# Mixture of experts: the first block for counts over 64 is computed third instead of second

## The chip, the cores and the metric

The kernel runs on one core of a Trainium2 chip. The metric is the device time of one execution in microseconds (us), the median of several runs. One execution more was recorded by the hardware profiler; the rows below come from it. The engines are TensorE (PE: matmuls and transposes), VectorE (DVE), ScalarE (ACT), GpSimd (POOL) and SyncE (SP); SP and POOL each issue transfers into a queue of their own, and 16 DMA engines serve both.

## The reference, cut to what matters

Two blocks of a language model run one after the other on 512 tokens of 1024 features. The change touches one part of the second, the mixture of experts. Each token goes to the 2 best of 8 experts of its best group, of 32 experts in all; an expert is a small gated network with 256 hidden features.

```python
def hierarchical_moe(h, w_rg, b_rg, w_re, b_re, w_gate, w_up, w_down):
    hf = h.reshape(-1, d)
    ...
    expert_id = g_sel[:, None] * EXPERTS_PER_GROUP + top_i
    combine = jnp.sum(jax.nn.one_hot(expert_id, N_EXPERTS, dtype=jnp.float32)
                      * (g_w * top_p)[..., None], axis=1)
    y = jnp.zeros_like(hf)
    for grp in range(N_GROUPS):
        sl = slice(grp * EXPERTS_PER_GROUP, (grp + 1) * EXPERTS_PER_GROUP)
        hid = jax.nn.silu(jnp.einsum('td,edf->tef', hf, w_gate[sl])) * jnp.einsum('td,edf->tef', hf, w_up[sl])
        y = y + jnp.einsum('tef,efd->td', hid * combine[:, sl, None].astype(hid.dtype), w_down[sl])
    return y.reshape(b, s, d)
```

## The kernel before

512 tokens with 2 experts each are 1024 pairs. The kernel sorts them by expert and gathers all their rows into `xs` before the first expert (four times two gathers `rows_a`, `rows_b`). The expert stage then works on windows of 64 pairs (`SLOTS`). Two windows are computed together as one step, one in each half of TensorE's output: a *main* step n computes the first 64 pairs of expert n and of expert n + 16. If an expert has more than 64 pairs, the rest goes into a block of an *over* step; over step o holds blocks o and o + 8 of a list that is filled from the front. For the inputs here two experts have more than 64 pairs (17 with 65, 19 with 67), so block 0 (in over step 0) and block 1 (in over step 1) are real, both in the first half of their step, and the other 14 are empty. All 24 steps are always run: 16 main ones (`M0` to `M15` below) and 8 over ones (`O0` to `O7`). `STEPS` is their order: M0 O0 M1 M2 O1 M3 M4 O2 M5 and so on.

A step s has these parts. `up(s)` multiplies the window with gate and up weights, in two halves c = 0 and c = 1 that have a weight panel each per window; ACT and DVE make the hidden rows from it (`xsg`, `xhid`), `turn_hid(s)` turns them with two transposes, ACT copies them (`xturn`), and `down_moe(s)` multiplies with the down weights (c = 2). ACT copies the result into `y_out`, which has two buffers, and POOL's `store_y(s)` scatters it to DRAM. TensorE's order is up(s), down(s - 1), turn(s); only at the start it is up(0), up(1), turn(0), down(0), turn(1).

The weights come as panels of 1 MB (128 x 2048 floats). Main panels, six per main step, come through SP's queue into a ring of nine buffers, in the order `PANEL_ORDER` that `_panel_order` builds from `STEPS`: the four up panels of step s, then the two down panels of step s - 1. The first nine are loaded before the stage begins; after that SP waits before panel n until `main_used` counts n - 8 panels used, so panel n takes the place of panel n - 9. Panel numbers start from 0.

Over panels come through POOL's queue, as indirect loads, one per half: `load_over(q)` with q = 3 * o + c loads part c of over step o for both halves into the buffer pair q % 2. For q of 2 and more it first waits for `over_used` to reach 2 * q - 2, that is until part q - 2 has been used. For an empty block only one row is in bounds, and the other rows are skipped. POOL executes its waits, loads and stores strictly in their written order. Before the stage it issues loads 0 and 1; then, after the table `y_row` is ready, the order that the change rewrites. ACT waits before it writes `y_out` of step s until the store of step s - 2 has landed.

After the last step POOL gathers the results (`back`), and the last part of the block follows.

Of the kernel before, what the change touches and what calls it, by code (L numbers as in the profile page):

```python
# [42 lines left out]
XOVER = 16  # L43
# [5 lines left out]
NO_WEIGHT = 16384  # L49


STEPS = [(kind, n) for o in range(XOVER // 2) for kind, n in (("main", 2 * o), ("over", o), ("main", 2 * o + 1))]
NSTEP = len(STEPS)
PANELS = 9


def _panel_order():

    up_at, down_at, order = {}, {}, []
    for s in range(NSTEP + 1):  # L60
        if s < NSTEP and STEPS[s][0] == "main":
            up_at[s] = len(order)
            order += [(STEPS[s][1] + XHALF * half, c) for c in range(2) for half in range(2)]
        if s and STEPS[s - 1][0] == "main":
            down_at[s - 1] = len(order)
            order += [(STEPS[s - 1][1] + XHALF * half, 2) for half in range(2)]
    return up_at, down_at, order
# [9 lines left out]
def column(s):  # L77

    kind, n = STEPS[s]
    return n if kind == "main" else XHALF + n  # L80
# [118 lines left out]
def build(nc, x_t, p_t, w_p, w_a, w_b, w_m, small, const, rope, decay, distance, out_t):  # L199
    ctx = ExitStack()  # L200
    with ctx:
# [2940 lines left out]
        def _(pool):  # L3142
# [80 lines left out]
            def load_over(q):  # L3223

                o, c = q // 3, q % 3
                if q >= 2:
                    pool.wait_ge(over_used, 2 * q - 2)
                for half in range(2):
                    j = half * (XOVER // 2) + o
                    pool.indirect_dma_start(  # L3230
                        over_panel[half][q % 2][:, :], None, w_m.rearrange("a p n -> (a p) n"),
                        bass.IndirectOffsetOnAxis(ap=over_row[:, c, j:j + 1], axis=0),
                        bounds_check=3 * EXPERTS * P - 1, oob_is_err=False).then_inc(over_loaded[half][q % 2], 16)

            def store_y(s):
                c = column(s)
                pool.wait_ge(y_copied, s + (2 if s == NSTEP - 1 else 1))
                pool.indirect_dma_start(
                    y_dram[:, :], bass.IndirectOffsetOnAxis(ap=y_row[:, c:c + 1], axis=0), y_out[:, s % 2, :], None,
                    bounds_check=PAIRS + XBLOCKS - 1, oob_is_err=False).then_inc(y_stored[s % 2], 16)  # L3240
# [16 lines left out]
            load_over(0)  # L3257
            load_over(1)
            pool.wait_ge(tables_ready, 5)
            for s in range(NSTEP):  # L3260
                kind, o = STEPS[s]
                if kind == "over":
                    load_over(3 * o + 2)
                    if o + 1 < XOVER // 2:
                        load_over(3 * o + 3)
                    store_y(s - 1)
                    if o + 1 < XOVER // 2:
                        load_over(3 * o + 4)
                    store_y(s)
                    store_y(s + 1)  # L3270
            pool.wait_ge(xwa_ready, NSTEP)
            pool.wait_ge(xwb_ready, NSTEP)
            for v in range(2):
# [208 lines left out]
```

## Time and profile before

| | |
|---|---|
| median of 3 runs | 2145.59 us (2143.97 to 2146.25) |
| profiled execution: time | 2143.46 us |
| profiled execution: span, first to last instruction | 2141.6 us |
| mean granted TensorE clock | 0.998 of full speed |
| busy: PE, PE weight load, DVE, ACT, POOL | 98%, 74%, 59%, 39%, 13% |
| expert stage, first up to last down | 1791.9 to 2062.9 us |

The time of the profiled execution is to be compared with its span: 1.9 us lie outside the recorded instructions. All times in rows are us from the start of the span. Matmuls are pipelined, so the end of one can lie behind the start of the next, and a few records of matmuls are missing (an up of 16 matmuls shows as 32 records of passes). In the expert stage L1413 is the matmul of `up`, L1424 that of `turn_hid`, L1437 that of `down_moe`, L3230 the load of an over panel and L3238 the store of a result.

### The profile page before, as it was taken

Reading aid. Unit: us, or ns where it says so; the run is one execution under the profiler, and the core shown is the slowest. Engines: PE = TensorE matmul, PEld = TensorE weight load, DVE = VectorE, ACT = ScalarE, POOL = GpSimd, SP = SyncE. Lnnn points to the kernel's source line nnn. Section 1 sums busy time; section 2 is a strip of 40 time slices with the busy share of each in tenths; the row PEclk is TensorE's granted clock in tenths of the full one; section 3 lists DMA queues with packets and bytes.
Section 4 is the critical chain, followed back from the end, with each engine's and each line's share of the span. In section 5 each row is a group of like instructions: output and inputs, shape, how many; then the busy total and the mean of one; then the engine's idle time right before and its main releaser. Section 6 shows DMA issues by size and latency. Waiting matters only on the chain.

```text
span 2141.6 us, 27223 instructions
## 1 busy us (share of the span) xinstructions
PE 2095.6 (98%) x10474; PEld 1578.0 (74%) x10474; DVE 1267.6 (59%) x1704; ACT 836.0 (39%) x1258; POOL 271.3 (13%) x234
## 2 busy tenths in 40 slices
PE   8999999999999999999999999999999998999998
PEld 6787788888878877888888888877778884333346
DVE  7887855555587678875655555588775454000038
ACT  6556522222253445774422222264552232122143
POOL 1334200000010064000100000020000023222220
PEclk9999999999999999999999999999999999999999
DMA  5322322223214352112322222221122158999961
GB/s 204 123 95 73 118 97 100 88 88 118 78 64 155 124 170 79 36 40 89 131 99 104 91 88 93 93 71 62 65 99 90 68 232 323 418 414 398 395 235 60
DMA packets 62622, 298.13 MB, mean 139 GB/s; under 512 B 14080, under 2 KB 14464, under 8 KB 34582
## 3 DMA queue, kind: packets, MB, share of 16 engines
q1 hardware_dynamic: 42560, 261.60, 31.9%
q0 software_dynamic: 19552, 34.55, 5.2%
q8 instruction: 63, 1.03, 0.2%
q10 hardware_dynamic: 416, 0.70, 0.1%
q14 instruction: 31, 0.25, 0.0%
HBM read 326.37 MB, written 22.48 MB: 163 GB/s over the span
## 4 chain that ended last, share of the span: by engine, by line
PE 79%; DVE 9%; DMA 6%; ACT 3%; issue 2%; POOL 1%; POOLq 0%; ACTq 0%; DVEq 0%
PE psum L652 21%; PE psum L654 21%; PE psum L653 21%; PE psum L1413 5%; DMA panel<-w_m 4%; PE psum L1437 3%; PE psum L1102 2%; PE psum L1077 1%; DVE a_lo L2137 1%; ACT a_hi L1520 1%; DMA over_panel<-w_m,over_row 1%; DVE xc L2294 1%; DVE hs L2248 1%; ACT hn_hi L1547 0%; PE psum L1235 0%
## 5 line engine op out<-in xcount | busy, mean ns | idle before, releaser
L652 PE MATMUL psum<-hn_hi,a_hi 128*128 128x512 f32 (+1 forms) x1592 | 628.4, 395 | 1.9 <-DVE a_lo L2126 0.9
L654 PE MATMUL psum<-hn_hi,a_lo 128*128 128x512 f32 (+1 forms) x1592 | 618.7, 389 | 0.0
L653 PE MATMUL psum<-hn_lo,a_hi 128*128 128x512 f32 (+1 forms) x1592 | 618.4, 388 | 0.0
L652 PEld LDWEIGHTS psum<-hn_hi,a_hi 128*128 128x128 f32 (+1 forms) x1592 | 297.2, 187 | 74.0 <-issue 8.2
L653 PEld LDWEIGHTS psum<-hn_lo,a_hi 128*128 128x128 f32 (+1 forms) x1592 | 297.4, 187 | 64.8 <-issue 2.4
L654 PEld LDWEIGHTS psum<-hn_hi,a_lo 128*128 128x128 f32 (+1 forms) x1592 | 297.0, 187 | 64.3
L2137 DVE TENSOR_TENSOR a_lo<-a_raw,a_hi 128x2048 fp32r<-128x2048 f32 (+2 forms) x108 | 247.3, 2290 | 69.4 <-ACT a_hi L1520 68.9
L1520 ACT ACTIVATE a_hi<-a_raw 128x2048 fp32r<-128x2048 f32 (+2 forms) x108 | 201.4, 1866 | 71.0 <-PE psum L654 61.8
L2236 DVE TENSOR_TENSOR h<-h,psum 128x512 f32<-128x512 f32 x176 | 119.4, 687 | 78.4 <-PE psum L654 78.4
L3150 POOL TENSOR_TENSOR sq<-sq 128x512 f32<-128x512 f32 x5 | 7.8, 1555 | 1121.6 <-ACT sq L1533 1121.6
L3072 DVE TENSOR_TENSOR xhid<-xsg,psum 128x256 f32<-128x256 f32 x24 | 10.1, 422 | 231.3 <-ACT xsg L2081 231.3
L1701 ACT ACTIVATE sg<-sg 128x512 f32<-128x512 f32 x44 | 27.8, 633 | 286.3 <-DVE sg L2407 286.3
L652 PE MATMUL psum<-hid_hi,b_hi 128*128 128x512 f32 x352 | 137.3, 390 | 2.2 <-DVE h L2236 2.1
L654 PE MATMUL psum<-hid_hi,b_lo 128*128 128x512 f32 x352 | 137.0, 389 | 0.0
L653 PE MATMUL psum<-hid_lo,b_hi 128*128 128x512 f32 x352 | 137.0, 389 | 0.0
L1413 PE MATMUL psum<-panel,xw 128*64 128x512 f32 x512 | 113.4, 595 | 0.0
L2412 DVE TENSOR_TENSOR hid<-sg,psum 128x512 f32<-128x512 f32 x44 | 30.3, 688 | 113.8 <-PE psum L654 113.6
L1703 ACT ACTIVATE hid_hi<-hid 128x512 fp32r<-128x512 f32 x44 | 27.8, 632 | 177.5 <-DVE hid L2412 177.5
L1527 ACT ACTIVATE b_hi<-b_raw 128x1024 fp32r<-128x1024 f32 x64 | 67.0, 1051 | 65.4 <-PE psum L654 63.2
L1413 PEld LDWEIGHTS psum<-panel,xw 128*64 128x64 f32 x512 | 35.3, 137 | 66.9 <-issue 66.5
L2143 DVE TENSOR_TENSOR b_lo<-b_raw,b_hi 128x1024 fp32r<-128x1024 f32 x64 | 79.8, 1254 | 1.0 <-ACT b_hi L1527 1.0
L652 PEld LDWEIGHTS psum<-hid_hi,b_hi 128*128 128x128 f32 x352 | 66.1, 188 | 17.5 <-issue 2.6
(533 smaller groups left out, 3257.2 us busy)
## 6 DMA issues: line engine op xcount, KB each, us to landing
a_raw<-w_a SPq DMA_DIRECT2D x115, 1024.0 KB, 5.1
panel<-w_m SPq DMA_DIRECT2D x96, 1024.0 KB
b_raw<-w_b SPq DMA_DIRECT2D x64, 512.0 KB, 3.4
q_scratch<-q_hi POOLq DMA_DIRECT2D x7, 384.0 KB
q_scratch<-qb_lo POOLq DMA_DIRECT2D x7, 384.0 KB
q_hi<-q_scratch POOLq DMA_DIRECT2D x7, 384.0 KB
q_lo<-q_scratch POOLq DMA_DIRECT2D x7, 384.0 KB
token_rows<-nat POOLq DMA_DIRECT2D x4, 512.0 KB, 5.4
```

The costliest lines, as they stand in the source:

```text
L652: pe.matmul(out, w_hi, x_hi, start=first, stop=False)
L653: pe.matmul(out, w_hi, x_lo, start=False, stop=False)
L654: return pe.matmul(out, w_lo, x_hi, start=False, stop=last)
L1102: mm = pe.matmul(bank[6 + at % 2][side * DV:(side + 1) * DV, t * P:(t + 1) * P], w, x, start=i == 0, stop=i == len(steps) - 1)
L1413: mm = pe.matmul(bank[v][rows, :], xw[:, v, k, rows], w[half][:, k % 4 * 2 * EFF:(k % 4 + 1) * 2 * EFF], start=k == 0, stop=k == KT - 1)
L1437: mm = pe.matmul(bank[4 + 2 * v + hb][rows, :], xturn[:, v, f * P + half * SLOTS:f * P + (half + 1) * SLOTS], w[half][:, f * D + hb * 512: ...
L1520: act.activation(a_hi[s % 2][:, 0:w], a_raw[s % 2][:, 0:w], ACT.Copy).then_inc(a_rounded, 1)
L1527: act.activation(b_hi[s % 2][:, :], b_raw[s % 2][:, :], ACT.Copy).then_inc(b_rounded, 1)
L2137: V.tensor_tensor(a_lo[s % 2][:, 0:w], a_raw[s % 2][:, 0:w], a_hi[s % 2][:, 0:w], ALU.subtract) \
L2143: V.tensor_tensor(b_lo[s % 2][:, :], b_raw[s % 2][:, :], b_hi[s % 2][:, :], ALU.subtract) \
L2236: V.tensor_tensor(h[:, m, :], h[:, m, :], bank[4 + m % 4][:, :], ALU.add).then_inc(y_free, 1)
L2412: V.tensor_tensor(hid[:, f, :], sg[:, f, :], ps[1][:, :], ALU.mult).then_inc(tile_free, 2)
```

## The change

The first over step comes as the third step of the stage, after M0 and M1, and no longer between them. The order becomes M0 M1 O0 M2 O1 M3 M4 O2 and so on: all other steps keep their places. The order of the main panels follows from `STEPS`. POOL's order is written anew, since the stores no longer come in threes: every load keeps its place relative to its over step (loads 3o + 2 and 3o + 3 before the store of the step ahead of it, load 3o + 4 behind that store), and the stores are counted up in between. All rows are still gathered before the first step.

```diff
-STEPS = [(kind, n) for o in range(XOVER // 2) for kind, n in (("main", 2 * o), ("over", o), ("main", 2 * o + 1))]
+STEPS = [("main", 0), ("main", 1), ("over", 0)] + [
+    (kind, n) for o in range(1, XOVER // 2) for kind, n in (("main", 2 * o), ("over", o), ("main", 2 * o + 1))]
 NSTEP = len(STEPS)
 PANELS = 9
@@
             load_over(0)
             load_over(1)
             pool.wait_ge(tables_ready, 5)
-            for s in range(NSTEP):
-                kind, o = STEPS[s]
-                if kind == "over":
-                    load_over(3 * o + 2)
-                    if o + 1 < XOVER // 2:
-                        load_over(3 * o + 3)
-                    store_y(s - 1)
-                    if o + 1 < XOVER // 2:
-                        load_over(3 * o + 4)
-                    store_y(s)
-                    store_y(s + 1)
+            over_at_step = [s for s in range(NSTEP) if STEPS[s][0] == "over"] + [NSTEP + 1]
+            at = 0
+            for o in range(XOVER // 2):
+                s, following = over_at_step[o:o + 2]
+                while at < s - 1:
+                    store_y(at)
+                    at += 1
+                load_over(3 * o + 2)
+                if o + 1 < XOVER // 2:
+                    load_over(3 * o + 3)
+                store_y(at)
+                at += 1
+                if o + 1 < XOVER // 2:
+                    load_over(3 * o + 4)
+                while at < following - 1:
+                    store_y(at)
+                    at += 1
```

POOL's order at the start was, after loads 0 and 1: load 2, load 3, store M0, load 4, store O0, store M1, load 5, load 6, store M2, load 7, store O1, store M3. It becomes: store M0, load 2, load 3, store M1, load 4, store O0, load 5, load 6, store M2, load 7, store O1, store M3.

## Rows read from the trace of the kernel before

**Rows 1.** The page: span, chain that ended last by line, issues of main panels.
```profile
span 2141.6 us, 27223 instructions
...
PE psum L652 21%; PE psum L654 21%; PE psum L653 21%; PE psum L1413 5%; DMA panel<-w_m 4%; PE psum L1437 3%; PE psum L1102 2%; PE psum L1077 1%; DVE a_lo L2137 1%; ACT a_hi L1520 1%; DMA over_panel<-w_m,over_row 1%; DVE xc L2294 1%; DVE hs L2248 1%; ACT hn_hi L1547 0%; PE psum L1235 0%
...
panel<-w_m SPq DMA_DIRECT2D x96, 1024.0 KB
```

**Rows 2.** Expert stage by windows: stretch, PE busy (records), PE clock, DMA share, GB/s.
```profile
1791.90:2062.90 271.00, 261.64 (x1202) 1.00 0.96 389
```

**Rows 3.** Timeline of PE, expert stage: start, length, line, what, [idle before <-releaser].
```profile
1791.88 7.09 PE L1413 MATMUL psum<-panel,xw 128*64 128x512 f32 x32
1798.80 3.60 PE L1413 MATMUL psum<-over_panel,xw 128*64 128x512 f32 x16
1802.94 3.65 PE L1413 MATMUL psum<-over_panel,xw 128*64 128x512 f32 x16 [0.54 <-DMA over_panel<-w_m,over_row]
1806.53 0.44 PE L1424 MATMUL psum<-cn,xhid 128*128 128x128 f32 x2
1807.44 3.65 PE L1437 MATMUL psum<-panel,xturn 128*64 128x512 f32 x16 [0.47 <-ACT xturn L2052]
...
1818.31 3.60 PE L1437 MATMUL psum<-over_panel,xturn 128*64 128x512 f32 x16
...
1833.03 7.09 PE L1413 MATMUL psum<-over_panel,xw 128*64 128x512 f32 x32
...
1843.85 7.09 PE L1413 MATMUL psum<-panel,xw 128*64 128x512 f32 x32
...
1856.01 7.09 PE L1413 MATMUL psum<-panel,xw 128*64 128x512 f32 x32
...
1897.46 3.65 PE L1437 MATMUL psum<-panel,xturn 128*64 128x512 f32 x16 [1.91 <-DMA panel<-w_m]
...
2032.45 3.65 PE L1437 MATMUL psum<-panel,xturn 128*64 128x512 f32 x16 [1.42 <-DMA panel<-w_m]
```

**Rows 4.** Waits of PE in the expert stage: us in total, times, longest.
```profile
PE psum L1437 <- DMA panel<-w_m: 6.2, 5, 1.9
```

**Rows 5.** DMA queues from 1791.9 to 1897.4: packets, MB, share of 16 engines.
```profile
q1 hardware_dynamic: 4756, 34.71, 79.3%
```

**Rows 6.** DMA queues from 1791.9 to 2032.4 (q1 is SP's queue, q0 POOL's).
```profile
q1 hardware_dynamic: 11895, 86.69, 87.2%
```

**Rows 7.** DMA queues from 1842 to 1847.
```profile
q1 hardware_dynamic: 148, 1.08, 51.6%
q0 software_dynamic: 148, 1.04, 49.8%
```

**Rows 8.** DMA queues from 1847 to 1850.
```profile
q0 software_dynamic: 165, 0.04, 6.5%
```

**Rows 9.** Chain that ended last, at M3: start, us, what.
```profile
1838.89 13.03 DMA over_panel<-w_m,over_row
```

**Rows 10.** DMA queues from 1838 to 1842.
```profile
q0 software_dynamic: 131, 0.38, 23.9%
```

**Rows 11.** Timeline of POOL: issues of loads (L3230) and stores (L3238), with idle before.
```profile
1793.64 0.99 POOL L3230 DMA_INDIRECT over_panel<-w_m,over_row  x1 [0.30 <-issue]
...
1813.01 1.02 POOL L3238 DMA_INDIRECT expert_out<-y_out,y_row  x1 [2.75 <-ACT y_out L2062]
...
1822.75 1.01 POOL L3230 DMA_INDIRECT over_panel<-w_m,over_row  x1 [8.71 <-PE psum L1437]
...
1834.63 1.00 POOL L3238 DMA_INDIRECT expert_out<-y_out,y_row  x1 [8.23 <-ACT y_out L2062]
...
1837.55 1.04 POOL L3230 DMA_INDIRECT over_panel<-w_m,over_row  x1 [1.92 <-PE psum L1413]
```

**Rows 12.** Timeline of PE at an idle stretch of another stage.
```profile
1452.48 0.88 PE L1224 MATMUL psum<-wpt,sv 128*64 128x128 f32 x12 [2.33 <-ACT wpt L1934]
```

**Rows 13.** Windows just behind it: PE busy (records), PE clock, DMA share, GB/s.
```profile
1453.50:1456.50 3.00, 3.00 (x11) 0.50 0.01 3
```

## The prediction, made before the change was run

> **What bounds the kernel now.** I read four views in this order: the page, the expert stage's windows and PE timeline, the waits, and the DMA queues by stretch. The page shows a kernel that TensorE fills; panels enter the last chain with 4% and over panels with 1% (span 2141.6 us) [rows 1]. The change touches only the expert stage. It lasts 271.0 us at full clock, with DMA at 0.96 of its time [rows 2]: TensorE and the weight stream are nearly even there. I call the main steps M0 to M15 and the steps for counts over 64 O0 to O7. A step has an up (two halves, c0 and c1), a turn and a down; PE's order is up of a step, down of the one before, turn. An undisturbed step is 10.82 us (O1's up at 1833.03, M3's at 1843.85), of which the up is 6.92 (1791.88 to 1798.80) and the rest 3.90 [rows 3]. 24 such steps are 259.7 us, so the stage loses 11.3 us. 6.2 of them are five waits for main panels, each before the down of an odd main step from M5 to M13 [rows 4].
>
> Which DMA engine is waited for matters. Panel 39 (M5's last; the first nine are loaded beforehand) ends the wait at 1897.46, when the queue has moved 34.71 MB, 33.1 panels of 1024 KB or 1.049 MB, though 39 is only the 31st. At 2032.45 it is the 79th, and 86.69 MB, 82.7 panels, have moved [rows 1, 3, 5, 6]. So a panel counts as landed when the last of the 16 engines is through, two to four panels behind the mean. That last engine needs 135.0 us for 48 panels, 2.81 each or 33.75 per three steps; PE needs 32.46.
>
> **The change, part by part.** *Same work.* No matmul, panel or over block is added; panels 4 to 15 only change places. Panels 4 to 7 become M1's, wanted early and already loaded. The queue goes on with panel 9 at about 1798.5, behind two over loads (2.1 MB, 5 us). At 2.81 us each, panel 9 (M0's down) is there by 1801.5, 11 (M1's down) by 1807, 15 (M2's up, with a store between) by 1820; they are wanted at 1806.6, 1817.5 and 1824.9: no wait. The wait of 0.54 in O0's up goes, since these loads landed at 1802.94 at the latest and O0's up now begins at 1810.6 [rows 3]. I cost it by the starts: M0's down follows its turn by 0.91 as before (1806.53 to 1807.44), and the turn begins at 1798.80 + 6.92 = 1805.72. So M0's down is at 1806.63, O0's up at 1810.58, M1's down at 1817.50, M2's up at 1821.40, O0's down due at 1828.32. With no wait M3's up would stand at 1843.04, 0.8 before its old start.
>
> *The move squeezes the over buffers.* O0 and O1 now have one main step between them, not two. Load q waits until load q-2 has been used. Loads 2, 3 and 4 (O0's c2, O1's c0 and c1) matter. Load 4 takes the buffer of load 2, which is free only after O0's down. That down now stands directly ahead of O1's up, which wants load 4 in its second half, 3.5 us after it begins. Before, M2's up lay between (load 4 was issued at 1822.75, wanted at 1836.5). So a load of 1.05 MB must come inside 4 us, and behind the others on POOL's queue.
>
> What a load costs with main panels queued is shown by load 5. Its full half (O1's first half is a real block, so the block is not empty and the move does what it says) moves 1.04 MB in 5 us while the main queue moves 1.08 [rows 7]; its empty half of small packets takes 3 us more [rows 8]; it lands at 1851.92, 1.9 after that [rows 9]. So 8 us of the queue, 10 to landing. The output store ahead of it, issued at 1834.63, moved 0.38 MB from 1838 to 1842 [rows 10, 11]. The issues follow PE: a store 5.57 us after its down's start (1807.44, 1813.01), a load waiting for a down 4.44 after its start (1818.31, 1822.75), one waiting for c0 4.52 after the up's start (1833.03, 1837.55), one waiting for c1 3.5 later [rows 3, 11]. All of POOL's DMAs up to there:
> - store of M0: issued 1812.2, data to 1820;
> - load 2: issued 1815.1, data 1820 to 1828, landed 1830. O0's down waits 1.7 us;
> - load 3: issued 1818.6, data to 1836, landed 1838. O1's up, due at 1833.9, waits 4 us; c0 ends at 1841.5;
> - store of M1: issued before load 4 now, data to 1840;
> - load 4: issued 1830 + 4.44 = 1834.4, data to 1848, landed 1850. c1 waits 8.5 us.
>
> The other sizing takes issue to landing of load 5 as it stands, 14.4 us [rows 9, 11]: O0's down at 1829.5, load 4 issued at 1833.9 and landed at 1848.3. The lower bound is the load that met no main panels: issued 1793.64, in use at 1802.94, 9.3 us [rows 3, 11]. Above, I allow 3 us more, as a load behind three others is not in the trace.
> The Trainium skill (DMA: Bandwidth & Descriptors, Anatomy of one DMA — SWDGE) puts such a DMA at about 2.0 us plus its bytes over 436e3. That would be an estimated 4.4 us, and load 4 would land at 1838.8; the trace disagrees, with 9.3 and 14.4, and the result by the page is a rival below.
>
> The main queue does stay full: panels 9 to 24 are 16.8 MB, three over loads and two stores 3.9, together 49 us at the 424 GB/s of [rows 7], from about 1798.5 to 1847. Panel 25 must wait for M2's down. Behind PE the ACT and DVE steps of O1, and POOL's store of O0 and load 5, slide along; nothing else waits for them.
>
> *From the landing on:* c1 3.5, M2's down and turn 3.9, so M3's up is at 1857.4 against 1843.85: +13.6. An idle PE also loses its clock: after 2.33 us without work it ran at 0.50 of full, 1.2 instead of 2.4 GHz, for over 3 us, at least 1.5 us of work lost [rows 12, 13]. The cost here is between 0 and 3.5; I take 2: +15.6.
>
> *What is given back.* The waits behind M3's up go while the weights are ahead. Before, M3's up to M4's took 12.16 instead of 10.82 (load 5, 1.34 lost); M4's up to M13's down took 176.44 instead of 15 x 10.82 + 6.92 = 169.22 [rows 3]. That is 8.56 in all. Can the last engine serve it? Panel 25 is issued at about 1859.5, data 2 us later; panel 39 lands at 1861.5 + 15 x 2.81 = 1903.7. PE wants it at 1859.4 + 50.2 = 1909.6. The lead of 6 us shrinks by 1.29 per three steps and at M13 is 0.7: just enough. The end is then that of before.
>
> Sum: 15.6 - 8.6 = +7.0; with the shorter sizing +5.3. I take +6.4, nearer the first, as load 4 has more ahead of it than load 5 had. Against the profiled execution (span 2141.6, time 2143.46, so 1.9 around it) this is 2149.9; its time lies 2.1 below the median of the runs, 2145.59, on which I put the difference: **2152.0 us**.
>
> **Rivals.** By the same sum the result is the landing of load 4 less 1843.0; it decides.
> *The load comes early (not slower).* If the queue serves it as it served the first loads, O0's down is not late, load 4 is issued at 1832.8 and lands at 1842.1. M3's up is at 1849.5, 5.7 us late and 7.7 with the clock, less than the 8.6 that PE gets back. The last DMA engine, which has work until about 1851 (16 panels by 2.81 and three loads by 2.5 from 1798.5) and gets panel 25 before that, is never idle, does the same work as before and sets the end: 2145.6, within 1 us. It holds from a landing before 1847.3 (+4.3). For it: main panels could run low on some engines. Against it: load 5's 14.4 with a shorter queue ahead.
> The page's formula leads here too: load 4 at 1838.8, and no difference.
> *Nothing is given back late.* If the last engine doesn't hold its lead beyond M5, only 1.34 and the 2.07 between M4's up and M5's down (41.45 against 3 x 10.82 + 6.92) return: 15.6 - 3.4 = +12.2, 2157.8 [rows 3]. For it: the lead of 0.7 at M13 is thin. Against: DMA was busy for 0.96 of the stage only [rows 2], so 2.81 per panel may hold idle time.
> *Faster.* The early waits gone (0.8) and the later ones too, would need load 4 within 4.3 us of its issue and a last DMA engine that gains: -4.3 at best, 2141.
>
> **Chances.** Forecast's case (+3.5 to +9) 0.56, early load 0.24, little given back 0.16, faster 0.04. 0.2% is 4.3 us, about what a measurement can tell from no change. Slower by more: most of the forecast's case and all of the third, 0.69; within: 0.27; faster 0.04. The range takes in the early load's edge and the third case: 2146 to 2158.
>
> **What would show it.** Right: PE idle 1 to 3 us before O0's down, then some 3 to 5 us before O1's c0 and 6 to 10 before its c1, both waits ended by an over panel; a stretch at 0.50 clock there; DMA share well below 1 for some 5 us just before panel 25; no wait for a main panel at M5 and M7, or small ones; the stage 277 to 278 us. Wrong: c1 waits less than 4 us; waits of over 1 us for main panels remain at M5 to M13; or new ones appear at M1's or M2's down, which I cost at nothing.

## The result

The changed kernel takes 2150.45 us (median of 6 runs, 2149.93 to 2152.07), the kernel before 2144.39 us in 6 runs on the same chips (2141.10 to 2146.25). The ratio is 1.0034, with a 95% interval of 1.0024 to 1.0043: slower by 6 us by the medians and by 7 us by the ratio. The forecast was 2152.0 us, or +6.4 us, with a range from 2146 to 2158.

The page of the profiled execution (2150.17 us), its span and the chain by line:

```profile
span 2148.4 us, 27223 instructions
...
PE psum L653 21%; PE psum L654 21%; PE psum L655 21%; PE psum L1414 7%; PE psum L1438 4%; PE psum L1103 2%; PE psum L1078 1%; DVE a_lo L2138 1%; DMA over_panel<-w_m,over_row 1%; DMA panel<-w_m 1%; ACT a_hi L1521 1%; DVE xc L2295 1%; PE psum L649 1%; PE psum L1463 1%; DVE hs L2249 1%
```

All lines of the code stand one lower than before (up is L1414, turn L1425, down L1438, over load L3231, store L3239). The chain now hardly goes over main panels (1% after 4%) [rows 1]. The whole difference lies in the expert stage, here as windows:

```profile
1792.20:2069.60 277.40, 264.40 (x1202) 0.98 0.94 380
```

It was 271.0 us at clock 1.00 and DMA share 0.96 [rows 2]. The timeline of PE shows where the time goes:

```profile
1792.18 13.95 PE L1414 MATMUL psum<-panel,xw 128*64 128x512 f32 x64
...
1810.92 7.09 PE L1414 MATMUL psum<-over_panel,xw 128*64 128x512 f32 x32
...
1829.56 3.65 PE L1438 MATMUL psum<-over_panel,xturn 128*64 128x512 f32 x16 [0.73 <-DMA over_panel<-w_m,over_row]
...
1837.06 5.35 PE L1414 MATMUL psum<-over_panel,xw 128*64 128x512 f32 x16 [3.47 <-DMA over_panel<-w_m,over_row]
1848.31 5.42 PE L1414 MATMUL psum<-over_panel,xw 128*64 128x512 f32 x16 [5.90 <-DMA over_panel<-w_m,over_row]
...
1857.47 7.09 PE L1414 MATMUL psum<-panel,xw 128*64 128x512 f32 x32
...
1868.29 7.09 PE L1414 MATMUL psum<-panel,xw 128*64 128x512 f32 x32
...
1907.66 3.60 PE L1438 MATMUL psum<-panel,xturn 128*64 128x512 f32 x16
...
2039.26 3.65 PE L1438 MATMUL psum<-panel,xturn 128*64 128x512 f32 x16 [1.23 <-DMA panel<-w_m]
...
2065.97 3.65 PE L1438 MATMUL psum<-panel,xturn 128*64 128x512 f32 x16 [1.06 <-ACT xturn L2053]
```

The rows are the ups of M0 and M1 together, O0's up, O0's down, the two halves of O1's up, M3's up, M4's up, M5's down, M13's down and M15's down. The stage begins 0.30 us later than before (1792.18 against 1791.88), which is taken off in what follows. M3's up is then 13.3 us late, M4's up 12.0, M5's down 9.9 and M13's down 6.5 [rows 3]; M15's down is 6.5 late too (it was at 2059.17). Three waits and a low clock cost 14.1 us, less the 0.8 us by which an undisturbed M3 would now come earlier, hence 13.3. Half of it is given back: 1.3 us by the wait for load 5 at M3's down, which is gone, and 5.5 us by the waits for main panels, of which one of the five is left [rows 3, 4]. In the waits of PE over the stage:

```profile
PE psum L1414 <- DMA over_panel<-w_m,over_row: 9.4, 2, 5.9
...
PE psum L1438 <- DMA panel<-w_m: 1.2, 1, 1.2
PE psum L1438 <- DMA over_panel<-w_m,over_row: 0.7, 1, 0.7
```

The timeline of POOL, with the store of M0, the first halves of loads 2 and 3, the store of M1 and the first halves of loads 4 and 5:

```profile
1812.61 1.02 POOL L3239 DMA_INDIRECT expert_out<-y_out,y_row  x1 [16.39 <-ACT y_out L2063]
1815.41 1.01 POOL L3231 DMA_INDIRECT over_panel<-w_m,over_row  x1 [1.79 <-PE psum L1414]
...
1818.84 1.00 POOL L3231 DMA_INDIRECT over_panel<-w_m,over_row  x1 [1.11 <-PE psum L1414]
...
1823.36 1.03 POOL L3239 DMA_INDIRECT expert_out<-y_out,y_row  x1 [2.22 <-ACT y_out L2063]
1834.02 1.01 POOL L3231 DMA_INDIRECT over_panel<-w_m,over_row  x1 [9.63 <-PE psum L1438]
...
1843.21 1.01 POOL L3231 DMA_INDIRECT over_panel<-w_m,over_row  x1 [5.54 <-PE psum L1414]
```

Load 4 is held back 9.63 us by O0's down and goes out at 1834.02, beside O1's up that wants it. The windows of PE around the two waits (stretch, PE busy, clock, DMA share, GB/s):

```profile
1838.00:1840.00 2.00, 2.00 (x8) 0.57 1.04 434
...
1846.00:1848.00 2.00, 0.00 (x0) 0.50 1.01 404
...
1850.00:1852.00 2.00, 2.00 (x8) 0.52 0.60 234
1852.00:1854.00 2.00, 2.00 (x12) 1.00 0.08 29
1854.00:1856.00 2.00, 2.00 (x12) 1.00 0.00 0
...
1858.00:1860.00 2.00, 2.00 (x12) 1.00 0.74 258
```

The clock is at 1.2 GHz behind the wait of 3.47 us and again in and behind that of 5.90 us, and each half of O1's up takes 5.3 us where it took 3.5. The Trainium skill (TensorE: Matmul & The Clock Gate, Why this matters for your kernels) warns of such idle gaps between bursts of matmuls; this trace agrees. DMA is nearly idle from 1852 to 1858: the main ring is full up to panel 24, and panel 25 waits for M2's down, as forecast. SP issues panel 25 at 1857.2.

### The profile page after: what moved, and what is told of

Its sections match the earlier page's. It is cut to its first block, busy times and chain, and to the rows that moved or that the text cites. A ratio compares the mean times of both kernels' runs of the same rounds, so it can differ in the third digit from the quotient of the medians.

```text
span 2148.4 us, 27223 instructions
## 1 busy us (share of the span) xinstructions
PE 2099.1 (98%) x10474; PEld 1579.8 (74%) x10474; DVE 1266.9 (59%) x1704; ACT 835.7 (39%) x1258; POOL 270.9 (13%) x234
## 4 chain that ended last, share of the span: by engine, by line
PE 82%; DVE 9%; ACT 3%; DMA 3%; issue 2%; POOL 1%; ACTq 0%; DVEq 0%; POOLq 0%
PE psum L653 21%; PE psum L654 21%; PE psum L655 21%; PE psum L1414 7%; PE psum L1438 4%; PE psum L1103 2%; PE psum L1078 1%; DVE a_lo L2138 1%; DMA over_panel<-w_m,over_row 1%; DMA panel<-w_m 1%; ACT a_hi L1521 1%; DVE xc L2295 1%; PE psum L649 1%; PE psum L1463 1%; DVE hs L2249 1%
## 5 line engine op out<-in xcount | busy, mean ns | idle before, releaser
L1414 PE MATMUL psum<-panel,xw 128*64 128x512 f32 x512 | 113.2, 595 | 0.0
L1414 PEld LDWEIGHTS psum<-panel,xw 128*64 128x64 f32 x512 | 35.4, 137 | 67.2 <-issue 66.9
```

Source lines behind the costliest of these rows:

```text
L1414: mm = pe.matmul(bank[v][rows, :], xw[:, v, k, rows], w[half][:, k % 4 * 2 * EFF:(k % 4 + 1) * 2 * EFF], start=k == 0, stop=k == KT - 1)
```

## Experiments

Every kernel was timed beside the kernel before. "Stage" is the distance from M0's up to M15's down in the profiled execution.

| kernel | median, us | ratio to before (95%) | stage, us |
|---|---|---|---|
| before | 2143.4 to 2144.4 | 1 | 267.3 |
| changed | 2150.45 | 1.0034 (1.0024 to 1.0043) | 273.8 |
| halves_out | 2146.22 | 1.0009 (1.0000 to 1.0018) | 268.9 |
| halves_out_free4 | 2142.26 | 0.9993 (0.9984 to 1.0002) | 267.1 |
| halves_out_free234 | 2140.72 | 0.9986 (0.9977 to 0.9995) | 264.8 |
| before_halves_out | 2141.15 | 0.9989 (0.9980 to 0.9998) | 264.6 |
| warm_wait | 2157.47 | 1.0066 (1.0052 to 1.0079) | 280.4 |
| warm_wait2 | 2148.80 | 1.0023 (1.0014 to 1.0032) | 272.6 |
| hold_main | 2148.75 | 1.0024 (1.0015 to 1.0034) | 272.6 |
| two_between | 2156.29 | 1.0061 (1.0047 to 1.0075) | 279.4 |
| no_empty_before | 2136.05 | 0.9966 (0.9952 to 0.9979) | 259.2 |
| no_empty_after | 2143.41 | 0.9997 (0.9988 to 1.0006) | 267.4 |

The queue theory: the over loads are late, as POOL's queue serves them one after the other, sharing the DMA engines with the main panels. Its rival, the buffer theory: load 4 is late by its buffer alone, with a fixed time from issue to landing. Further rivals: the new order of the main panels costs, or the clock does, or the giving back is a coincidence.

### Queue or buffer: four kernels without the empty second halves

`halves_out` leaves out the second halves of loads 0 to 5 (the blocks are empty, and TensorE computes them with the first half's panel). `over_into` returns None for these halves:

```diff
                 for half in range(2):
+                    b = over_into(q, half)
+                    if b is None:
+                        continue
                     j = half * (XOVER // 2) + o
```

> The changed kernel without the loads of the empty second halves of O0 and O1 (loads 0 to 5; TensorE reads the first half's panel in their place, and rows of empty blocks are not stored). Queue theory (POOL's DMAs to the over buffers are served one after the other at half rate beside main panels, an empty half costing 3 us): load 2 lands before 1828, load 3 before 1833, so the waits of 0.7 and 3.5 us go; load 4, issued at about 1833, lands at about 1843, and its wait is 6 to 7 us from a start 4 us earlier; M3's up at 1850 to 1851.5 instead of 1857.5; time 2144 to 2146.5. Buffer theory (a fixed 14.2 us from issue to landing, and the issue waits for the buffer): load 4 lands at 1847, M3's up at 1854 to 1855, 2147 to 2148.5. If the empty halves cost nothing: as the changed kernel, 2150.5.

Measured: loads 2 and 3 cause no wait any more; the one for load 4 is left:

```profile
1833.18 3.65 PE L1437 MATMUL psum<-over_panel,xw 128*64 128x512 f32 x16
1843.49 6.13 PE L1437 MATMUL psum<-over_panel,xw 128*64 128x512 f32 x16 [6.66 <-DMA over_panel<-w_m,over_row]
```

O1's c0 starts 4.5 us earlier than in the changed kernel and load 4 is used 5.4 us earlier, both from M0's up. It was issued at 1833.71 and used 9.8 us later, not 14.3: the empty halves, its own and those ahead of it in the queue, have a price. The fixed time of the rival is refuted. M3's up is 1 us later than the queue theory had it, since c1 ran at the low clock and took 6.0 us; the time of 2146.22 us lies in that theory's range.

In `halves_out_free4` load 4 goes to the free second-half buffer and waits for nothing:

```diff
+OVER_PLAN = {4: (2, None)}
```

> As halves_out, and load 4 goes to a buffer of its own (that of the left-out second half), so it is issued right behind the store of M1 at about 1824.5 instead of 1833. Buffer theory: the landing moves by the same 8 to 9 us, no wait in O1's second half, M3's up at 1844. Queue theory: its data can only begin when load 3 and the store of M1 are through, about 1834; landed at about 1841, a wait of 3.5 to 5 us, M3's up at 1847 to 1849. Time in both 2143.5 to 2146, as the last DMA engine sets the end; clearly below before (under 2142) would say that it does not.

Measured: POOL issues it 32.5 us after M0's up and no longer 40.9, thus 8.4 us earlier; PE uses it at 47.8 and no longer 50.7, thus 2.9 us earlier.

```profile
1823.12 1.01 POOL L3257 DMA_INDIRECT over_panel<-w_m,over_row  x1 [0.30 <-issue]
```
```profile
1838.40 6.57 PE L1437 MATMUL psum<-over_panel,xw 128*64 128x512 f32 x16 [3.74 <-DMA over_panel<-w_m,over_row]
```

From issue to use it now takes 15.3 us. So the wait for load 4's own buffer is worth 2.9 us here, and a wait of 3.74 us is left that the buffer theory had at nothing: loads 2 and 3, issued as late as in `halves_out`, are still ahead. The time of 2142.26 us is 1 us below what either theory expected. A kernel that has a spare buffer and the second halves as well wasn't tried.

In `halves_out_free234` loads 2 and 3 are issued at 1804, before the store of M0, into buffers of their own, and load 4 behind O0's c0:

```diff
+OVER_PLAN = {2: (2, None), 3: (3, None), 4: (0, 2), 5: (1, 4)}
```

> As halves_out, with buffers for loads 2 and 3 that are free from the start (issued at about 1805, as in the kernel before) and load 4 waiting only for O0's first half (issued at about 1815). Both theories: no wait for an over panel, M3's up at 1843 to 1844, so the whole loss is gone: 2143 to 2145.5. If instead the new order of the main panels cost something of its own, waits for main panels appear at M1's or M2's down and the time stays over 2146.

Measured: no wait for an over panel at all. M3's up is 51.2 us behind M0's, where it is 65.3 in the changed kernel and 52.0 in that before: the 0.8 us that the walk put on the new order are there. The order of the main panels is that of the changed kernel, so it isn't what costs. Nor is the place of O0 by itself: what costs is that loads 2, 3 and 4 are issued too late. Five waits for main panels are back, 5.8 us in all. The time was expected at 2143 to 2145.5 us and is 2140.72. `before_halves_out` is the control, the old order with the same halves left out.

> The kernel before, with the same second halves left out as in halves_out (loads 0 to 5), as the control for the three kernels of that name. Loads 0 and 1 land 1 us earlier and load 5 some 3 us earlier, so the waits of 0.54 and 1.1 go. If the last DMA engine sets the pace, 6 of 44 empty issues less give 1 to 1.5 us: 2142 to 2143.5. Then halves_out_free234 (2140.7) is 1 to 2.5 us faster by the new order alone, in which O0's loads have more time; if the new order were worth nothing, this one comes out at 2140.7 as well.

Measured 2141.15 against 2140.72, stages of 264.6 and 264.8 us. The expectation of 2142 to 2143.5 was too high, and the rival named in it holds: with the loads in time, the place of O0 is worth nothing either way. The 0.8 us early are lost again to main panels. The gain of 2 to 3 us against the kernel before comes from the halves left out, which both kernels share.

### Clock: dummy matmuls in the waits

`warm_wait` puts dummy matmuls ahead of the waits of O1's two halves:

```diff
                     if k % 4 == 0:
+                        if s == 4:
+                            pe.wait_ge(xturn_done, 4)
+                            keep(3, 32 if k else 10)
                         w, used = weights(s, k // 4)
```

> The changed kernel with dummy matmuls (10 and 32 of 128x256) ahead of the two waits of O1's up, so that TensorE is not idle in them. Clock theory: both halves of O1's up take 3.5 us instead of 5.3 and 5.2; the first is hidden by the second's wait, so M3's up comes 1.7 us earlier (1855.8), and so does the request for panel 25; time 2148.5 to 2149.5. If the end hangs on something else, M3's up is earlier but the time stays at 2150.5 and the waits for main panels grow by 1.7. Should the dummy matmuls outlast the wait: up to 1 us later.

Measured: 7 us slower than the changed kernel. A dummy is two records of 0.22 us, and 32 of them last far beyond the landing:

```profile
1841.63 14.08 PE L649 MATMUL psum<-cn 128*128 128x256 f32 x64
1855.64 3.65 PE L1417 MATMUL psum<-over_panel,xw 128*64 128x512 f32 x16
```

The size was wrong, not the idea; both halves of the up take 3.5 us. `warm_wait2` has 5 and 15 in their place.

> As warm_wait, with 5 and 15 dummy matmuls instead of 10 and 32: in warm_wait a dummy took 0.44 us, not 0.22, and 32 of them 14 us, so that TensorE came 8 us too late to load 4. Now 2.2 and 6.6 us, inside the waits. Clock theory: both halves of O1's up at 3.5 us, c0 starting within 0.5 us of the landing of load 3, M3's up 1.5 to 1.8 us earlier than in the changed kernel, time 2148.5 to 2149.5. If the end hangs on something else: 2150.5.

```profile
1840.98 6.74 PE L649 MATMUL psum<-cn 128*128 128x256 f32 x30
1848.83 3.65 PE L1417 MATMUL psum<-over_panel,xw 128*64 128x512 f32 x16 [1.10 <-DMA over_panel<-w_m,over_row]
...
1856.22 7.09 PE L1417 MATMUL psum<-panel,xw 128*64 128x512 f32 x32
```

Load 4 lands at the same time, M3's up comes 1.5 us earlier (63.8 behind M0's) and the stage is 1.2 us shorter. The interval of its ratio overlaps with that of the changed kernel; its middle is 0.0011 lower. The trace shows the low clock as a term of about 1.5 us; the times alone don't set it clear of noise.

### Sharing: main panels held back

`hold_main` lets SP wait before panel 19 until load 4 has landed:

```diff
+                if n == 19:
+                    for half in range(2):
+                        sp.wait_ge(over_loaded[half][0], 16 * 3)
```

> The changed kernel, but SP issues no main panel from number 19 on until load 4 has landed, so that POOL's loads have the DMA engines alone from about 1829. Queue theory: load 3 lands 2 to 3 us sooner, load 4 within 8 to 9.5 us of its issue (instead of 14.2), so its wait is under 2 us; but 4 to 6 panels come late, with waits of 5 us and more at M3's up, and DMA stands idle: 2150 to 2156. If the loads' time doesn't depend on main panels: load 4's wait stays near 6 us, and the late panels add to it: over 2156.

```profile
1834.08 1.02 POOL L3234 DMA_INDIRECT over_panel<-w_m,over_row  x1 [9.56 <-PE psum L1441]
```
```profile
1839.95 3.65 PE L1417 MATMUL psum<-over_panel,xw 128*64 128x512 f32 x16 [2.72 <-DMA over_panel<-w_m,over_row]
```

From issue to use load 4 takes 5.9 us where it took 14.3, less than the 8 to 9.5 expected; its wait of 2.72 us is more than the 2 expected. Load 3's wait is gone. Behind the wait of 2.72 us c1 takes 3.5 us: the granted clock stayed at 1.00, where it fell behind 2.55 us in `two_between` below and behind 2.33 us in [rows 12, 13]. The price is paid later (a wait of 1.5 us at M3's c1 and six of 7.4 us in all before downs), but smaller than expected: at 2148.75 us it is no slower than the changed kernel, perhaps 2 us faster.

### Spacing: two main steps between all over steps but the last two

```diff
-STEPS = [("main", 0), ("main", 1), ("over", 0)] + [
-    (kind, n) for o in range(1, XOVER // 2) for kind, n in (("main", 2 * o), ("over", o), ("main", 2 * o + 1))]
+STEPS = [(kind, n) for o in range(XOVER // 2 - 1) for kind, n in (("main", 2 * o), ("main", 2 * o + 1), ("over", o))] + [
+    ("main", XOVER - 2), ("over", XOVER // 2 - 1), ("main", XOVER - 1)]
```

> The changed kernel with the next over steps moved as well: M0 M1 O0 M2 M3 O1 and so on to M12 M13 O6, then M14 O7 M15. Two main steps stand again between O0 and O1; the squeeze is now between O6 and O7, whose loads are empty in both halves. My theory: no wait in O1's up, only a small one (0 to 5 us) before O7's second half, as empty loads take 3 us each and few are queued; time 2143.5 to 2147. Rival, that the third place of O0 or the new order of the panels costs: 2149 to 2151 as the changed kernel. Rival, that squeezed over steps cost whatever they load: a wait of 8 us and more at O7, at the end where nothing is given back, 2150 to 2156.

Measured 2156.3: my expectation missed by 9 us. The first half held: no wait in O1's up. But M4's second half waited 2.55 us for a main panel. In this order it needs panels 26 and 27, in the other two 24 and 25, since here M3's down panels stand ahead of it; that this is the reason wasn't tested. Six waits for main panels before downs, 5.4 us in all, stayed. And O7, squeezed against O6, waited 7.0 us, though all its loads are empty:

```profile
2049.81 5.70 PE L1414 MATMUL psum<-over_panel,xw 128*64 128x512 f32 x16 [7.00 <-DMA over_panel<-w_m,over_row]
```
```profile
2036.00:2040.00 4.00, 4.00 (x20) 1.00 0.99 401
2040.00:2044.00 4.00, 2.81 (x14) 1.00 0.86 344
2044.00:2049.50 5.50, 0.00 (x0) 0.79 0.10 29
```

The windows show what the wait is for. From 2044 to 2049.5 the mean share of the 16 engines is 0.10, little above one engine's 0.06, and 29 GB/s are moved. Near its end the DMA queues look like this (GB/s in 40 slices of 0.05 us, then q1, SP's, and q0, POOL's):

```profile
GB/s 164 0 0 0 0 0 164 0 0 0 0 0 164 0 0 0 0 0 0 164 0 0 0 0 0 164 0 0 0 0 0 82 0 0 164 0 0 0 0 0
...
q1 hardware_dynamic: 6, 0.05, 5.8%
q0 software_dynamic: 6, 0.00, 0.6%
```

From 2048 to 2050 one packet of 8 KB of a main panel passes every 0.3 us, and as many tiny ones of POOL's queue. At the share of a single engine, this can be read as one engine that works off what the others finished about 5 us before, with load 22, issued at 2039.69, waiting for it. So the rival named in the expectation, that squeezed over steps cost whatever they load, is nearly what happened: a wait of 7.0 us and 2156.3 us, where it had 8 us and more and 2150 to 2156.

### What the empty loads cost, and what is given back

`no_empty_before` and `no_empty_after` leave out all empty loads but those of loads 0 and 1 (40 of 42; the expectations count 38 of 44), in the old and in the new order. TensorE still computes every step, with what the buffers hold:

```diff
+def left_out(q, half):
+    o = q // 3
+    return q >= 2 and (half == 1 or o >= 2)
...
                 for half in range(2):
+                    if left_out(q, half):
+                        continue
```

> The kernel before without any empty load but those of loads 0 and 1 (no over load at all from O2 on, no second half in O0 and O1). My theory that the last of the 16 DMA engines sets the pace (2.81 us per panel, small packets taking turns with panel packets): the 38 empty issues take their share from it, the rate falls to 2.6 to 2.7 us per panel, below the 2.70 that TensorE allows, and the five waits for main panels before M5 to M13 shrink from 6.2 us to under 2: 2137.5 to 2141. Rival, that the waits come from the depth of the ring: they stay, 2143 to 2145, but for the 1.3 us of load 5.

> The same on the changed kernel. Load 4's wait falls as in halves_out (M3's up at about 1851), and if the last DMA engine is quicker without empty loads, no wait for a main panel is left behind it and TensorE sets the end: M3's up is 8 us late and 8.5 of waits are gone against the kernel before, 2143 to 2145; against the kernel before without empty loads it would be 4 to 7 slower. If the engine's pace isn't changed: 2145 to 2147.

In the old order no wait for a main panel is left; the stage falls from 267.3 to 259.2 us, which is TensorE's own pace but for a wait of 1.07 us in O0's up. The kernel is 7 us faster though the left-out loads carry almost no bytes, more than expected (2136.05 us, not 2137.5 to 2141). The ring is as deep as before, so its depth wasn't the reason for the waits. In the new order PE waits once for a DMA:

```profile
1843.25 6.16 PE L1424 MATMUL psum<-over_panel,xw 128*64 128x512 f32 x16 [6.77 <-DMA over_panel<-w_m,over_row]
```

This is the wait of `halves_out` (6.66 us). There it made the stage 4.3 us longer than in its control (268.9 against 264.6); here, where no other wait is left that could be given back, it makes it 8.2 longer (267.4 against 259.2). The kernels differ by 7.4 us (2143.41 against 2136.05), a little above the 4 to 7 expected.

## Why the prediction was right, point by point

- *What bounds the stage.* Right. The wait for the last DMA engine was read from two sums of bytes [rows 5, 6]; the packets of `two_between` bear it out, though no trace tells the engines apart. `no_empty_before` shows what the waits for main panels weigh: M4's up to M13's down falls from 176.4 us to PE's 169.2, so 7.2 of the 8.1 us of the stage, the rest being mostly load 5's wait.
- *Same work, no new wait for main panels at the start; O0's wait gone.* Right: O0's up is at 1810.62 after taking off 0.30, forecast 1810.58, and there is no wait until O0's down.
- *The walk through POOL's queue.* Right in mechanism, 0.7 to 2 us long in each term (all with 0.30 taken off): O0's down 0.9 late (forecast 1.7), load 3 used at 1836.8 (1838), load 4 issued at 1833.7 (1834.4) and used at 1848.0 (1850; by the shorter sizing 1848.3). 14.3 us from issue to use is within 0.2 of load 5's. The waits of PE came out at 0.73, 3.47 and 5.90 us; the first and the last lie a little under the ranges named for them (1 to 3 and 6 to 10). The 4.4 us by the formula of the Trainium skill (DMA: Bandwidth & Descriptors, Anatomy of one DMA — SWDGE) came nowhere near it; the 5.9 us of `hold_main`, without main panels, is nearest.
- *The name given to the cause.* "The move squeezes the over buffers" is right if all three loads are meant. In the kernels without the second halves, freeing load 4's buffer alone brought only 2.9 us of an issue 8.4 us earlier, while buffers for loads 2 and 3 and an earlier load 4 took the whole wait away: loads 2 and 3 were issued at 1815.4 and 1818.8 in the changed kernel where they went out at 1805.3 and 1807.9 before, and load 4 stands behind them. The main panels beside it are the other part: with them held back it took 5.9 us and not 14.3 (and load 3 was through earlier too). The Trainium skill (DMA: Bandwidth & Descriptors, Queues, rings and completion order) says that an engine takes turns between its rings, packet by packet; the 148 packets of either queue in [rows 7] agree.
- *Clock.* Forecast 2 us, 1.8 by the length of c1 (5.24 against 3.46), 1.5 by `warm_wait2`. The low clock in c0 cost nothing, since c0 ends before load 4 lands.
- *M3's up.* Forecast +15.6, measured +13.3: the landing was 2.0 us earlier than forecast and the clock 0.2 us cheaper.
- *What is given back.* Forecast 8.56, measured 6.8: all of it up to M5 (1.3 and 2.1), but 3.4 in place of 5.15 after it. The lead at M13, forecast 0.7 us, was negative: a wait of 1.23 us stayed there, by the prediction's own list a sign of being wrong. This term was too large by 1.8 us. From the issue of panel 25 at 1857.2 to M13's down there are 63 panels in 182.1 us; with the forecast's 2 us for the first data taken off that is 2.86 each, where 2.81 was assumed. Why the last engine was slower here isn't known.
- *Sum.* 13.3 - 6.8 = +6.5 against +6.4 (+7.0 by the walk). The mechanism was right, but that the number came so near is partly luck: a cost 2.3 us too large and a giving back 1.8 us too large cancel.
- *Rivals.* The load that comes early fell with a landing at 1848.0, above the bound of 1847.3. It was above it by 0.7 us only. "Nothing is given back late" held for a third of the stretch after M5 (3.4 of 5.15 us came back). "Faster" fell.

## What to carry to other kernels

A load that reuses a buffer is only as early as the use that frees it, and then stands in its queue behind everything issued before and beside everything in the other queue; so walk the queue from the profile (data rate under load, what is ahead, when it may be issued) before moving the consumer. A stall of one kind is worth less where stalls of another kind follow: what was behind catches up, and the price is the stall less what is given back; where nothing follows, it is the whole. Loads that move next to nothing can still cost (40 of them 8.1 us here). And a wait for a transfer can last while the mean DMA share is as low as 0.10, so the mean share doesn't show what the wait is for.

## What had not been expected of the hardware

The empty indirect loads, each with 127 rows out of bounds, move almost nothing (0.04 MB in 3 us) [rows 8], yet leaving out 40 of them takes 8.1 us off the stage. Near the end of `two_between`'s main panels, DMA went on for 5.5 us and more at about the share of a single engine. Which engine it is, this trace doesn't tell; the Trainium skill (DMA: Bandwidth & Descriptors, Latency and other measured facts) calls engines 7 and 15 usually slower and suspects the rings that hold the descriptors of GpSimd's transfers, a cause that no run here tested. A real load of 1 MB took 5.9 us from issue to use with an idle main queue, 9.8 with a full one but no empty halves, and 14.3 with a full one and all of them.
